# Stage boundaries of a fused two-model kernel: the last expert scatter issued in the next stage, five waits for stores placed at the first use of their data, semaphore clears on GpSimd

## What is computed

```python
# first block (one layer)
h  = modulate(rmsnorm(x, norm1_g), sh1, sc1);  p = h @ w_in
y_hy = hyena_mixer(p[..., :1536], ...)        # filters by rfft, two long convolutions
y_hg, _ = hgrn_mixer(p[..., 1536:], pc[..., 1536:], ...)   # chunked scans, chunks of 64
x = x + g1 * (concat([rmsnorm(y_hy), y_hg]) @ w_out)
h2 = modulate(rmsnorm(x, norm2_g), sh2, sc2)
# expert choice: each of 16 experts takes its top 128 tokens, y is added back at these rows
x = rmsnorm(x + g2 * ec_moe(h2, router_w, w1, w3, w2), final_g)
# second block (two layers): differential attention, a Fourier mix, a pooling mix
for l in range(2):
    x, ctx = mixer_layer(l, x, ctx, ...)      # p = h @ w_in; attention over 1280 keys; (y * silu(g)) @ w_out
```

## Time and profile before

| | us |
|---|---|
| median of 3 runs | 4081.03 (4079.36 to 4086.21) |
| the profiled execution | 4076.85 |
| its span, first to last instruction | 4075.1 |
| PE busy | 3715.1 (91%) |
| DVE busy | 2573.2 (63%) |
| ACT busy | 1898.4 (47%) |
| POOL busy | 799.7 (20%) |
| mean granted clock of PE | 0.962 |

### The profile page before, as it was taken

The page is one execution under the profiler, slowest core; times in us unless marked ns, Lnnn a source line. Parts: engine busy times, 40 slices in busy tenths (PEclk is TensorE's granted clock), DMA queues, the critical chain, the costliest instruction groups (busy, mean ns, idle before and its releaser), DMA issues. The chain is left out here.

```text
span 4075.1 us, 44172 instructions
## 1 busy us (share of the span) xinstructions
PE 3715.1 (91%) x17357; PEld 2889.7 (71%) x17357; DVE 2573.2 (63%) x2795; ACT 1898.4 (47%) x2499; POOL 799.7 (20%) x591
## 2 busy tenths in 40 slices
PE   7999898986778899999999998999898899998988
PEld 4887644446667388887878786778777577787857
DVE  5445364548956888888888887651376625515753
ACT  5211200047654376777777676451266314514731
POOL 2100034210012002121212111420144224202422
PEclk9999898998888999999999998999999999999999
DMA  5553315111043899999999998443420433435123
GB/s 193 203 181 128 113 67 189 54 69 45 27 151 146 291 368 369 383 368 376 370 379 365 372 379 287 142 130 115 172 94 14 156 125 120 135 108 198 52 93 119
DMA packets 389065, 779.10 MB, mean 191 GB/s; under 512 B 26168, under 2 KB 110003, under 8 KB 388600
## 3 DMA queue, kind: packets, MB, share of 16 engines
q1 hardware_dynamic: 366074, 699.46, 47.9%
q0 software_dynamic: 17856, 66.33, 4.9%
q10 hardware_dynamic: 4928, 10.49, 0.8%
HBM read 664.74 MB, written 111.48 MB: 190 GB/s over the span
## 5 line engine op out<-in xcount | busy, mean ns | idle before, releaser
L3012 DVE TENSOR_TENSOR moe_w_low<-shared_z,moe_w_high 128x2048 fp32r<-128x2048 f32 x256 | 594.0, 2365 | 92.7 <-ACT moe_w_high L2965 91.3
L2965 ACT ACTIVATE moe_w_high<-shared_z 128x2048 fp32r<-128x2048 f32 x256 | 476.8, 1914 | 175.4 <-DMA shared_z<-in_exp_w 168.7
L172 PE MATMUL moe_bank<-moe_w_high,moe_xgT_high 128*128 128x512 f32 x1024 | 404.5, 395 | 10.9 <-DVE moe_w_low L3012 5.9
L174 PE MATMUL moe_bank<-moe_w_high,moe_xgT_low 128*128 128x512 f32 x1024 | 399.9, 391 | 0.0
L173 PE MATMUL moe_bank<-moe_w_low,moe_xgT_high 128*128 128x512 f32 x1024 | 399.8, 390 | 0.0
L3012 DVE TENSOR_TENSOR moe_w_low<-moe_w_raw,moe_w_high 128x2048 fp32r<-128x2048 f32 x128 | 287.3, 2286 | 62.3 <-ACT moe_w_high L2965 61.7
L2965 ACT ACTIVATE moe_w_high<-moe_w_raw 128x2048 fp32r<-128x2048 f32 x128 | 238.3, 1910 | 116.4 <-DMA moe_w_raw<-in_exp_w 115.2
L3238 POOL TENSOR_SCALAR layer_att_p<-layer_att_p,layer_att_rinv,layer_att_neg_lam 128x1280 f32<-128x1280 f32 (+1 forms) x72 | 173.4, 2408 | 527.2 <-DVE layer_att_neg_lam L3267 313.4
L3245 DVE TENSOR_REDUCE layer_att_nb<-layer_att_scores 128x1 f32<-128x1280 f32 (+1 forms) x144 | 195.0, 1369 | 88.8 <-PE layer_att_scores L3150 87.7
L172 PE MATMUL layer_front_bank<-layer_front_w_high,layer_front_hT_high 128*128 128x512 f32 (+1 forms) x608 | 229.6, 378 | 7.9 <-POOL layer_front_hT_low L799 7.9
L172 PEld LDWEIGHTS moe_bank<-moe_w_high,moe_xgT_high 128*128 128x128 f32 x1024 | 192.9, 188 | 56.2 <-DVE moe_w_low L3012 9.9
(11 more groups left out here) (556 smaller groups left out, 8574.7 us busy)
## 6 DMA issues: line engine op xcount, KB each, us to landing
shared_z<-in_exp_w SPq DMA_DIRECT2D x128, 2048.0 KB, 10.3
moe_w_raw<-in_exp_w SPq DMA_DIRECT2D x64, 2048.0 KB, 10.3
shared_z<-in_w_in SPq DMA_DIRECT2D x48, 512.0 KB, 6.5
first_raw<-in_w_in SPq DMA_DIRECT2D x32, 512.0 KB, 7.5
front_vec<-in_ada_w POOLq DMA_DIRECT2D x16, 1024.0 KB, 5.9
late_raw<-in_w_mod SPq DMA_DIRECT2D x8, 2048.0 KB, 8.3
proj_t<-front_out SPq DMA_DIRECT2D x48, 256.0 KB, 2.2
shared_z<-in_w_out SPq DMA_DIRECT2D x12, 1024.0 KB, 6.1
```

Of the source, the lines that this page charges most:

```text
L172: nc.tensor.matmul(out, lhs[0], rhs[0], start=start, stop=False)
L174: return nc.tensor.matmul(out, lhs[1], rhs[0], start=False, stop=stop)
L2965: nc.scalar.activation(hi, x, ACT.Copy).then_inc(high, 1)
L3012: nc.vector.tensor_tensor(lo, x, hi.bitcast(F32), ALU.subtract).then_inc(low, 1)
```

## The change

1. The clears of retired semaphores are issued by POOL (`@block.gpsimd`) in place of SP, the same number at the same fifteen starts.
2. Five waits of SP for stores at the end of a stage are gone: those of the three fronts, of filter and of hgrn. A new helper, `core.stored`, waits for the same lanes in the next stage that reads the data or writes over the stored tiles: on SP ahead of the first load in filter (6 lanes) and in both att stages (8 lanes), on ACT in hyena ahead of its loads of the spectra, and on SP in mixout ahead of the loads of tile 1.
3. The scatter of the last expert is issued by POOL in layer0's front, behind the clears and ahead of `low_of`.
4. In filter the tables cos and sin are allocated ahead of the other tiles, so that of what lies over the front's output tiles nothing is written but by SP's loads.

```diff
+    def stored(self, eng, lanes):
+        for lane in lanes:
+            eng.wait_ge(lane.sem, lane.at(0))
...
             if retired:
-                @block.sync
-                def _(sp):
+                @block.gpsimd
+                def _(pool):
                     for s in retired:
-                        sp.sem_clear(s)
+                        pool.sem_clear(s)
             yield block
...
@@ stage_front, end of SP @@
-                for j in range(RS):
-                    sp.wait_ge(core.hstore[j].sem, core.hstore[j].at(len(range(j, len(plain), RS))))
-                for j in range(2 if R else 0):
-                    sp.wait_ge(core.hstore[RS + j].sem, core.hstore[RS + j].at(stores_of(j, R)))
...
@@ stage_front, start of POOL @@
                 if vectors:
                     sums.fill_pick(pool)
+                if space:
+                    core.last_scatter(pool)
                 for i in range(-2, N + 4):
...
@@ stage_filter: tiles, start and end of SP @@
         win, wave, w_in, skip = core.filter_in
+        tab = [st.sb("cos", [P, NT, SEQ // 2]), st.sb("sin", [P, NT, SEQ // 2])]
         wave_high, hs = st.sb("wave_high", [P, SEQ], F32R), st.sb("hs", [P, SEQ], F32R)
         w_fold = st.sb("w_fold", [P, 2, 2, HY])
         w_high, w_low = (st.sb(k, [P, 2, 2, HY], F32R) for k in ("w_high", "w_low"))
-        tab = [st.sb("cos", [P, NT, SEQ // 2]), st.sb("sin", [P, NT, SEQ // 2])]
...
+                core.stored(sp, core.hstore[0:6])
                 sp.dma_start(lag0[:, :], io["t_lag0"]).then_inc(windows, 16)
...
-                for j in range(RS):
-                    sp.wait_ge(core.hstore[j].sem, core.hstore[j].at(len(range(j, 2 * len(pairs), RS))))
...
@@ stage_hyena, ACT @@
                         place_u(1)
+                        core.stored(act, core.hstore[0:6])
                         for f in range(RSP):
                             act.dma_start(spec[f][:, :, :], core.spectra[0, :, f * P:(f + 1) * P, :].rearrange(
...
@@ stage_hgrn, end of SP @@
-                for j in range(4):
-                    sp.wait_ge(core.hstore[j].sem, core.hstore[j].at(H * NT // 4))
...
@@ stage_mix_norm (mixout), SP @@
                 load_w(1)
+                core.stored(sp, core.hstore[0:4])
                 tile(1)
...
@@ stage_moe, POOL @@
+        def last_scatter(pool):
+            pool.wait_ge(scattered, 16 * (E - 1))
+            pool.indirect_dma_start(out=core.x1, out_offset=bass.IndirectOffsetOnAxis(
+                ap=core.moe_idx[:, E - 1:E], axis=0), in_=yo[(E - 1) % 2][:, :], in_offset=None,
+                compute_op=ALU.add).then_inc(scattered, 16)
+        core.last_scatter = last_scatter
...
                     if e + 1 < E:
                         split_x(e + 1)
-                scatter(E - 1)
...
@@ stage_attend, start of SP @@
+                core.stored(sp, core.hstore[0:8])
                 sp.dma_start(lv[:, :, :], io["lam_vecs_2"][l].partition_broadcast(P)).then_inc(vectors, 16)
```

## The result

The change runs in 4060.85 us, the median of five runs (4055.03 to 4063.44), against 4081.2 for the kernel before (five runs, 4079.36 to 4086.21): 20.35 us less, ratio 0.9946 with a 95% interval of 0.9931 to 0.996, that is 16 to 28 us. I had said 4067 in a range of 4058 to 4076. A second set of five runs of the unedited change on another chip gave 0.9943 (0.993 to 0.9957). Direction and range held; the gain forecast, 14.3 us, lies just outside the interval on the small side.

What follows compares the result with a forecast made beforehand. PE, busy 91% of the span, left little inside stages, so the prediction counted stage boundaries: -1.3-2.5-1.5-2.3+0.6-5.5-1.5-1.9+1.6 = -14.3 us. From the median 4081.03 that gave 4066.7, stated as 4067, range 4058 to 4076.

Steps and rivals of the forecast that it cites:

- The method, boundary by boundary: At fifteen stage boundaries: which engine ended the old stage last, what the new one's first matmul awaited; terms sum to -14.3 us.
- Filter's cover: Filter's start: 27 clears (1.5 us) ahead of POOL's memsets stay hidden, since 2.5 us remain before the first matmul.
- A clear on POOL at SP's price: All stage starts: a clear on POOL costs SP's 0.056 us, since both are instructions without data.
- the rival built beside it: Clears on POOL cost 0.16 us each, delaying stages POOL leads: only -4.7 us, 4076; chance 0.10.
- the second one: Clears on POOL so dear the kernel gets slower: gain cancelled from 0.20 us each, 4091 at 0.27; chance 0.04.
- Moe's start, +0.6: Start of moe: eleven clears ahead of POOL's first gather delay the first expert matmul, a loss of 0.6 us.
- The scatter, -5.5, from -3.5 to -7.85: Moe to layer0's front: front starts 7.85 us earlier, partly lost waiting for x; range from slower landing to nothing lost.
- the landing of x: Layer0's front: SP's loads of x, issued at 2526.5, take 5.8 us to 2532.3; ACT waits 2.9 us for tile 2.
- The third rival: Layer0's front: scatter lands 4 us later beside DVE's work; boundary gives -1.5, -10.3 in all, 4071; chance 0.14.
- SP's earlier loads in hyena, hgrn and mixout: Without clears SP loads earlier: 1.0 us for hyena's fwd_add, -1.5 for hgrn's mask, -1.1 for mixout's w_out.
- Mix, +0.8 each: Att to mix, both layers: fourteen clears ahead of POOL's ones, which PE awaits, cost 0.8 us each, 1.6 together.
- the lower bound: Good end of all terms: -7.85 for the front, both mixes zero, att carrying 2.4 and 3.4; about -21 us, 4060.

## Why the prediction was right, and where it was not

- *The method, boundary by boundary.* It held. Starts came earlier by 1.4 (filter) and the like where a wait for stores was gone. Filter's cover held: its first matmul did not move against its start. Out's did not: I had put this stage at zero, since PE there waits for DVE's w_low and POOL's low parts end earlier, and its first matmul came 0.65 us later in both layers, by a slower DVE beside the later rows of POOL.
- *A clear on POOL at SP's price, 0.056.* 0.070 measured in three places, up to 0.093 in others. Right enough; the rule of the Trainium skill ("GPSIMD Engine Reference", section 3, Performance versus the Vector engine) on two software hops, read as 0.16 us or more a clear, does not hold for this instruction, and the rival built beside it is out, as is the second one, which needed 0.20 or more.
- *Moe's start, +0.6.* +0.78 at the gather. Right.
- *The scatter, -5.5, from -3.5 to -7.85.* Counted at ACT's tile 2 it was 8.05-1.3 = -6.8. The step that was off is the landing of x: 5.8 us taken, 3.8 from issue to ACT's start measured. The 5.8 of the earlier trace rows are the median of both tiles' loads, with final_g's 512 KB issued 0.4 us ahead of them; in the change the same two take 4.2. Counted to the end of the front, over all profiles, the move of the scatter is worth 3.9 us and not 6.8, so that -5.5 lies between the two counts. Alone, with final_g beside the scatter, the part is worth 0 to 9 us by time. The third rival (a scatter held up in the front) is half right: it happens, by 1.8 us, when a load goes out beside it, and in the change it goes out ahead. The rule of the Trainium skill named there ("SBUF - State Buffer", section SBUF: two separate sides) asks for an operation of DVE as the cause; moving a load alone took the delay away, with DVE's work unchanged.
- *SP's earlier loads in hyena, hgrn and mixout.* A term that was too small, by how much depends on the profiles taken. With clears alone hyena and hgrn gained 2.3 and 3.1 us where I counted 1.0 and 1.5; over the profiles with the waits moved it is 1.8 and 1.4. What hgrn gained beyond the mask is not traced to a wait; the granted clock of its last 25 us was 1.00 in seven of nine profiles with the clears on POOL and in one of five with them on SP, 0.93 in the others, which may be part of it.
- *Mix, +0.8 each.* Right in layer0 (77.88 to 79.05 and 78.88), wrong in sign in layer1 (67.73 to 64.88 and 65.41). The failed step is that a first matmul which waits longer for the ones makes the stage end later: in layer1 PE waits for DVE again, from 28 us after the start in the kernel before, and that wait took the delay up and, being shorter, kept the clock.
- *What I did not see at all:* filter's clock. Its sixteen matmuls were 2.7 us shorter in the profile of the change, 1.0 in the second one.
- *A slip in the working.* Att's loads come 0.5 and 28 clears of 0.056 earlier, 2.1 us, where I wrote 2.4, and the 3.4 of the lower bound is derived nowhere. Neither changes the forecast; with 2.1 twice, the bound would be about -19 and not -21.

So beside the 6 us by which the median gained more than my 14.3, the stage lengths of two profiles show 3.1 to 3.7 for layer1's mix (from +0.8 to -2.3 and -2.9), some 3 for hyena, hgrn and mixout together (1 by the means over the profiles), 1.0 to 2.7 for filter's clock and 1.3 for the scatter. These make more than 6; out's 0.65 twice, moe's chance and the front's stand against them, and the medians don't settle it finer.

## What to carry to other kernels

A wait at the end of a stage is paid by every engine, and it can be read as the time between the last useful row and the next stage's first; moving it to the first use of the data gave what those rows said, where SP had issued the stores. Where POOL had issued the last transfer, taking its wait away gave 0.6 us of 4.5: there the transfer itself has to go elsewhere, as the scatter did. Housekeeping cost a similar small price on either engine (0.056 and mostly 0.070 us a clear), so put it on the one that does not lead the stage; to know who leads, look past the first matmul to the next wait of PE, and at what a shifted row will then run beside. Ahead of a transfer that others wait for, see what other transfer goes out in the same microsecond.

## What was not expected of the hardware

- A gap of PE of 3.45 us, the same in each profile, was followed by sixteen matmuls of 7.13, 8.83 or 9.79 us, by the granted clock. In layer1's mix gaps of 3.9 us or more were followed by the lower clock each time, 2.7 us or less never, so that a first matmul a microsecond later made the stage 0.9 us shorter in one pair of kernels and 4.9 in another, 3.3 in the mean over all profiles.
- An indirect scatter of 128 rows landed in 6.2 us with a broadcast load issued 1.6 us ahead, in 8.0 to 8.4 with it 0.11 us behind, and in 6.4 with it held back.
- In the two places where POOL's last transfer went out on its own queue and no instruction waited for it, the next stage started only behind its landing: 8.35 us from the last row of DVE at moe's end, 3.91 at the end of out.
- Moe, at a DMA share of 0.9 and more, varied by 6 to 7 us between profiles of kernels with the same instructions in it, a third of the gain.
